# Three-block kernel on one core: the experts' weight chunks made whole and their ring one long strip, low parts of the dense weights written in place, the last dense loads on ScalarE's queue

## The reference, cut to what matters

```
hn = rmsnorm(h, ln_ffn[1])
logits = hn @ w_router;  top 2 of 8, softmax over the two -> combine[token, expert]
for e in range(8):
    g, u = split(hn @ w_gu[e])            # w_gu[e]: 1024 x 7168
    out += combine[:, e] * ((silu(g) * u) @ w_down[e])   # w_down[e]: 3584 x 1024
return rmsnorm(h + out, ln_final)
```

## Time and profile before

| | |
|---|---|
| median of 3 runs | 1381.46 us (1381.21 to 1382.87) |
| profiled execution, device time | 1384.53 us |
| its span, first to last instruction | 1382.8 us |
| TensorE / VectorE / ScalarE busy | 95% / 34% / 26% |
| DMA | 445.41 MB, mean 322 GB/s |
| mean granted TensorE clock | 0.990 |

### The profile page before, as it was taken

One profiled execution on the slowest core, in us unless ns is written; L12 is line 12 of the kernel. 1 busy time (PEld: TensorE's weight loads), 2 busy tenths in 40 slices (PEclk: granted clock), 3 DMA queues, 4 the chain that ended last, 5 costly groups with the idle time before them and its releaser, 6 DMA issues.

```text
span 1382.8 us, 29468 instructions
## 1 busy us (share of the span) xinstructions
PE 1320.2 (95%) x12866; PEld 804.5 (58%) x12866; DVE 471.6 (34%) x756; ACT 361.1 (26%) x524; POOL 37.7 (3%) x62
## 2 busy tenths in 40 slices
PE   9999999999999999999999998999988999988885
PEld 8678888887899987454345353345343345343242
DVE  7775555446689983320200200200200200200102
ACT  6754444335578853200000000000000000000001
POOL 1000000000002221000000000000000000000000
PEclk9999999999999999999999999999999999999997
DMA  9446555564644449899999999999999999999992
GB/s 351 135 153 213 183 184 182 184 203 130 201 134 126 150 183 369 350 424 425 425 425 424 424 424 425 424 425 425 423 426 425 423 425 424 425 425 426 421 424 116
DMA packets 112593, 445.41 MB, mean 322 GB/s; under 512 B 10400, under 2 KB 36272, under 8 KB 81744
## 3 DMA queue, kind: packets, MB, share of 16 engines
q1 hardware_dynamic: 109216, 440.44, 80.3%
q10 hardware_dynamic: 2912, 2.36, 0.5%
q0 software_dynamic: 336, 0.71, 0.2%
HBM read 442.43 MB, written 1.05 MB: 321 GB/s over the span
## 4 chain that ended last, share of the span: by engine, by line
PE 67%; SPq 14%; DMA 10%; DVE 4%; issue 2%; ACT 2%; DVEq 1%; ACTq 0%
PE bank L1302 22%; SPq L381 14%; PE bank L797 10%; PE bank L799 10%; PE bank L798 10%; PE bank L1318 9%; DMA e_ring<-moe_w_down_in 4%; DMA e_late<-moe_w_down_in 2%; DMA e_top<-moe_w_down_in 2%; DMA e_ring<-moe_w_gu_in 2%; PE bank L1292 1%; DVE w_lo L1441 1%; PE bank L1273 1%; ACT w_hi L504 1%; DVE acc L1777 1%
## 5 line engine op out<-in xcount | busy, mean ns | idle before, releaser
L1302 PE MATMUL bank<-e_ring,xgT 128*32 128x512 f32 (+1 forms) x3840 | 375.6, 540 | 8.8 <-DMA e_ring<-moe_w_gu_in 8.8
L1302 PEld LDWEIGHTS bank<-e_ring,xgT 128*32 128x32 f32 x3840 | 122.3, 110 | 251.8 <-issue 221.8
L1441 DVE TENSOR_TENSOR w_lo<-ring,w_hi 128x2048 fp32r<-128x2048 f32 (+1 forms) x84 | 191.8, 2288 | 108.3 <-ACT w_hi L504 108.0
L1318 PE MATMUL bank<-e_ring,m_hT 128*32 128x256 f32 x3344 | 194.6, 388 | 23.8 <-DMA e_ring<-moe_w_down_in 17.9
L504 ACT ACTIVATE w_hi<-ring 128x2048 fp32r<-128x2048 f32 (+1 forms) x84 | 158.9, 1894 | 127.5 <-PE bank L799 119.6
L1318 PEld LDWEIGHTS bank<-e_ring,m_hT 128*32 128x32 f32 x3344 | 111.8, 112 | 101.0 <-issue 28.9
L797 PE MATMUL bank<-w_hi,hT_hi 128*128 128x512 f32 (+1 forms) x336 | 130.7, 389 | 1.9 <-DVE w_lo L1441 1.9
L1998 DVE TENSOR_TENSOR m_sg<-m_sg,bank 128x512 f32<-128x512 f32 (+1 forms) x38 | 21.6, 617 | 321.8 <-PE bank L1302 321.8
L799 PE MATMUL bank<-w_hi,hT_lo 128*128 128x512 f32 (+1 forms) x336 | 129.2, 385 | 0.0
L798 PE MATMUL bank<-w_lo,hT_hi 128*128 128x512 f32 (+1 forms) x336 | 129.1, 384 | 0.0
L757 ACT ACTIVATE m_sg<-bank 128x512 f32<-128x512 f32 (+1 forms) x38 | 18.3, 543 | 374.1 <-PE bank L1302 374.1
(11 more groups left out here) (358 smaller groups left out, 1427.2 us busy)
## 6 DMA issues: line engine op xcount, KB each, us to landing
e_ring<-moe_w_gu_in SPq DMA_DIRECT2D x100, 1024.0 KB, 26.4
e_ring<-moe_w_down_in SPq DMA_DIRECT2D x88, 1024.0 KB, 24.5
e_ring<-moe_w_gu_in SPq DMA_DIRECT2D x101, 768.0 KB, 22.2
ring<-ffn_w_gu_in SPq DMA_DIRECT2D x28, 1024.0 KB, 5.1
ring<-ffn_w_down_in SPq DMA_DIRECT2D x14, 1024.0 KB, 4.9
e_top<-moe_w_gu_in SPq DMA_DIRECT2D x14, 1024.0 KB, 27.2
e_late<-moe_w_gu_in SPq DMA_DIRECT2D x14, 1024.0 KB, 26.9
e_top<-moe_w_down_in SPq DMA_DIRECT2D x12, 1024.0 KB, 24.4
```

Of the source, the lines that this page charges most:

```text
L1302: ins = pe.matmul(bank[banks[b]][quad_of(q), 0:w].rearrange("p (m v) -> p m v", v=P // 2), xgT[:, k, quad_of(b)], columns_of(e_slot(p * LA ...
L1318: ins = pe.matmul(bank[DOWN[b]][quad_of(q), 0:256], m_hT[:, 2 * c + k, rows], wv[:, columns], start=(c == 0 and k == 0), stop=(c == KT // ...
L1441: dve.tensor_tensor(w_lo[:, m % SPLIT, 0:w], ring[:, m % RING, 0:w], w_hi[:, m % SPLIT, 0:w].bitcast(F32), ALU.subtract).then_inc(lo_ready, 1)
```

## The change

Seven things change.

1. **Chunks of the experts.** A gate or up chunk is one whole row block, 128 x 3584 floats (14 KiB for each partition, 1.835 MB); a down chunk has four rows of 1024 for each partition (16 KiB, 2.097 MB). A pass has 23 chunks in place of 46: 8 gate, 8 up, 7 down.
2. **The ring.** One strip of 12 x 14 KiB = 168 KiB per partition in place of 19 x 8 KiB = 152 KiB. `expert_ring` lays the chunks end to end and notes for each the last chunk that it overwrites (`E_FREES`); 13 semaphores (`e_loaded`) follow the loads.
3. **The first lap.** Twelve chunks (22.0 MB) in place of 19 (19.1 MB). Their waits are others: three go after SyncE's last dense load, one at SO0, then at MOE0 - 5, MOE0 - 4 and MOE0 - 2, one once the norm is done, and the last four at MOE0, when TensorE has used the last dense chunk.
4. **The dense stage.** `w_lo` lies over `ring`, so that VectorE writes it in place, and a slot is reloaded after TensorE's use (`chunk_used`) and not after `w_lo`. The eight loads SO0 to MOE0 - 1 are issued by ScalarE in `ahead`, ahead of the rounding three chunks back.
5. **The order in a pass.** Each gate chunk goes through all banks of both sets, then each up chunk. Up goes over the gate banks, each once its silu is read (`m_silu`). `rows_next` stands ahead of `down`. `down` has banks of 512 columns.
6. **The start and the end.** The first expert matmul waits for all eight pieces of `xgT` (before: for the first four), and the last pass fills one bank of 512 columns per tile, copied in pieces of 32x512 (before: two banks, 32x256).
7. **Gains.** `ln_ffn` is loaded after MOE0 (before: before it), `ln_final` in the last pass (before: at 565 us).

```diff
+STRIP = 128
 SETS = ((0, 512), (4 * 512, 384))
-CONTIGUOUS = 15
-SLOT_OF = (17, 18, 13, 14, 15, 0, 1, 2, 3, 4, 5, 16, 6, 7, 8, 9, 10, 11, 12)
-ERING = len(SLOT_OF)
...
 KT = FF // P
-LAYER_CHUNKS = 32 + KT // 2
+GU_CHUNKS = 2 * KD
+DOWN_ROWS = 4
+LAYER_CHUNKS = GU_CHUNKS + KT // DOWN_ROWS
+FIRST_LAP = (2, 3, 4, 5, 6, 7, 8, 1, 9, 10, 11, 0)
+LANES = len(FIRST_LAP) + 1
+E_AT = 25600
+HT_AT = E_AT + len(FIRST_LAP) * 4 * FF - 96 * 1024
+
+
+def chunk_size(i):
+    return FF if i % LAYER_CHUNKS < GU_CHUNKS else DOWN_ROWS * D
+
+
+def expert_ring():
+    places, at, size = [], FIRST_LAP[0] * FF, len(FIRST_LAP) * FF
+    for i in range(ROUND_CHUNKS):
+        if i < len(FIRST_LAP):
+            places.append(FIRST_LAP[i] * FF)
+            continue
+        at = at if at + chunk_size(i) <= size else 0
+        places.append(at)
+        at += chunk_size(i)
+    frees = [max([i - LANES] + [j for j in range(i) if places[j] < places[i] + chunk_size(i)
+                                and places[i] < places[j] + chunk_size(j)]) for i in range(ROUND_CHUNKS)]
+    return places, frees
+
+
+E_PLACE, E_FREES = expert_ring()
...
+        def dense_load(queue, n):
+
+            width = sum(p[3] for p in stream[n])
+            for src, k, a, w in stream[n]:
+                dst = ring[:, n % RING, 0:k * width].rearrange("p (k n) -> p k n", n=width)
+                queue.dma_start(dst[:, :, a:a + w], src).then_inc(slot_loaded[n % RING], 16)
...
+        e_ring, = phase(E_AT, e_ring=((len(FIRST_LAP) * FF,), F32))
+        hT_hi, hT_lo, hT, ring, w_hi = phase(
+            HT_AT, hT_hi=((KD, T), F32R), hT_lo=((KD, T), F32R), hT=((KD, T), F32), ring=((RING, SLOT), F32),
+            w_hi=((SPLIT, SLOT), F32R))
+        _, _, decay_mov, decay_stat, after, ident_r, w_lo = phase(
+            HT_AT, under_hT_hi=((KD, T), F32), under_hT_lo=((KD, T), F32), decay_mov=((TT, REP, P), F32R),
+            decay_stat=((2, 3, P), F32R), after=((P,), F32R), ident_r=((P,), F32R), w_lo=((RING, SLOT), F32R))
...
-        GATE, UP, DOWN = (0, 1, 2), (3, 4, 5), (6, 7, 5)
-        FIRST_AT = [(6, 0), (5, 0), (5, 1), (4, 0), (4, 1), (4, 2), (3, 0), (3, 1)]
-        FIRST_DONE = (1, 2, 2, 3, 3, 3, 4, 4)
+        ROWS, DOWN = (0, 1), (6, 7)
+        FIRST_AT = [(6, 0), (5, 0), (5, 1), (5, 2), (2, 0), (2, 1), (2, 2), (2, 3)]
+        FIRST_DONE = (1, 2, 2, 2, 3, 3, 3, 3)
...
-            for n, pieces in enumerate(stream):
+            for n in range(SO0):
...
                 if n >= RING:
-                    sp.wait_ge(lo_ready, n - RING + 1)
-                for src, k, a, w in pieces:
-                    width = sum(p[3] for p in pieces)
-                    dst = ring[:, n % RING, 0:k * width].rearrange("p (k n) -> p k n", n=width)
-                    sp.dma_start(dst[:, :, a:a + w], src).then_inc(slot_loaded[n % RING], 16)
+                    sp.wait_ge(chunk_used, n - RING + 1)
+                dense_load(sp, n)
 
             def expert_load(e, i):
 
                 c = i % LAYER_CHUNKS
-                if c < 32:
-                    first, w = SETS[c // 16]
-                    a = c // 8 % 2 * FF + first
-                    src, n = block_of(moe_w_gu[0, e], c % 8, 1, a, BLOCKS * w), BLOCKS * w
+                if c < GU_CHUNKS:
+                    src = moe_w_gu[0, e][P * (c % KD):P * (c % KD + 1), c // KD * FF:(c // KD + 1) * FF]
                 else:
-                    rows = slice(2 * P * (c - 32), 2 * P * (c - 31))
-                    src, n = moe_w_down[0, e][rows].rearrange("(p k) n -> p k n", k=2), 2 * D
-                dst = e_slot(i)[:, 0:n].rearrange("p (k n) -> p k n", k=src.shape[1])
-                sp.dma_start(dst, src).then_inc(e_loaded[i % ERING][0], 16)
+                    rows = slice(DOWN_ROWS * P * (c - GU_CHUNKS), DOWN_ROWS * P * (c - GU_CHUNKS + 1))
+                    src = moe_w_down[0, e][rows].rearrange("(p r) n -> p (r n)", r=DOWN_ROWS)
+                sp.dma_start(e_slot(i), src).then_inc(e_loaded[i % LANES], 16)
 
...
                 sp.wait_ge(c_dt_parts, 4)
-                for i in range(2):
+                for i in range(3):
                     expert_load(0, i)
                 sp.wait_ge(chunk_used, SO0)
-                for i in range(2, 4):
-                    expert_load(0, i)
+                expert_load(0, 3)
+                sp.wait_ge(c_abx, G)
+                sp.wait_ge(chunk_used, MOE0 - 5)
+                expert_load(0, 4)
+                sp.wait_ge(chunk_used, MOE0 - 4)
+                expert_load(0, 5)
+                sp.wait_ge(chunk_used, MOE0 - 2)
+                expert_load(0, 6)
                 sp.wait_ge(c_y, G)
-                expert_load(0, 4)
-                for r in range(RING):
-                    sp.wait_ge(lo_ready, MOE0 + r - RING + 1)
-                    expert_load(0, 5 + r)
                 sp.wait_ge(c_yThi, KI)
                 sp.wait_ge(c_yTsb, KI)
                 sp.wait_ge(c_norm, 1)
-                expert_load(0, 5 + RING)
-                for r in range(2 * SPLIT):
-                    sp.wait_ge(chunk_used, MOE0 + r % SPLIT - SPLIT + 1)
-                    expert_load(0, 6 + RING + r)
-                sp.wait_ge(r_mm, 4)
-                expert_load(0, ERING - 1)
+                expert_load(0, 7)
+                sp.wait_ge(chunk_used, MOE0)
+                for i in range(8, len(FIRST_LAP)):
+                    expert_load(0, i)
...
-                    for i in range(max(p * LAYER_CHUNKS, ERING), (p + 1) * LAYER_CHUNKS):
-                        sp.wait_ge(chunk_used, it * ROUND_CHUNKS + (MOE0 + i - ERING + 1))
+                    for i in range(max(p * LAYER_CHUNKS, len(FIRST_LAP)), (p + 1) * LAYER_CHUNKS):
+                        sp.wait_ge(chunk_used, it * ROUND_CHUNKS + (MOE0 + E_FREES[i] + 1))
...
+                    if SO0 <= m + RING - SPLIT < MOE0:
+                        dense_load(act, m + RING - SPLIT)
...
+            act.wait_ge(chunk_used, MOE0)
+            act.dma_start(ffn_gain, ln_ffn[1].partition_broadcast(P)).then_inc(ffn_gain_loaded, 16)
...
-                def up_or_gate(c, s, banks):
-                    w, k = SETS[s][1], c % 8
+                def up_or_gate(c, passed, free=None):
+
+                    k, at = c % KD, hidden_banks(p)
                     have_e(c)
-                    for b in range(groups):
+                    for i, (s, b) in enumerate(at):
+                        if free and k == 0:
+                            pe.wait_ge(free, it * banks_before(E) + (banks_before(p) + i + 1))
                         for q in range(BLOCKS):
...
+                            ins = pe.matmul(hidden_bank(s, b)[quad_of(q)].rearrange("p (m v) -> p m v", v=STRIP),
+                                            xgT[:, k, quad_of(b)], columns_of(e_slot(p * LAYER_CHUNKS + c), s, q),
                                             start=(k == 0), stop=(k == KD - 1), tile_position=(0, q * QUAD))
+                        if k == KD - 1 and i < len(at) - 1:
+                            ins.then_inc(passed, 1)
                     ins.then_inc(chunk_used, 1)
 
...
+                def down(c):
+
+                    have_e(GU_CHUNKS + c)
+                    last = c == KT // DOWN_ROWS - 1
+                    for b in range(groups - 1):
+                        for r in range(DOWN_ROWS):
+                            wv = e_slot(p * LAYER_CHUNKS + GU_CHUNKS + c)[:, r * D:(r + 1) * D]
+                            for q in range(4):
+                                rows, columns = down_at(b, q)
+                                ins = pe.matmul(bank[DOWN[b]][quad_of(q), 0:columns.stop - columns.start],
+                                                m_hT[:, DOWN_ROWS * c + r, rows], wv[:, columns],
+                                                start=(c == 0 and r == 0), stop=(last and r == DOWN_ROWS - 1),
+                                                tile_position=(0, q * QUAD))
+                        if last and b < groups - 2:
                             ins.then_inc(m_y, 1)
-
+                    ins.then_inc(chunk_used, 1)
+
+                pe.wait_ge(xg_sb, it * (2 * E) + (2 * p + 2))
...
+                    up_or_gate(KD + k, m_up, m_silu)
                 if p == 0:
                     pe.wait_ge(rows_ready, TT)
                 pe.wait_ge(pass_sel, it * E + (p + 1))
-                pe.wait_ge(m_h, it * (2 * E) + (2 * p + 2))
+                pe.wait_ge(m_h, it * (2 * E) + (2 * p + 1))
                 rows_next()
-                for c in range(4, 8):
-                    down((c,))
+                if p == 0:
+                    pe.wait_ge(rows_held, it + 1)
+                else:
+                    pe.wait_ge(h_added, it * (2 * TT * E) + (2 * TT * p + 2 * TT))
+                pe.wait_ge(m_T, it * (2 * E) + (2 * p + 1))
+                for c in range(4):
+                    down(c)
                 pe.wait_ge(m_T, it * (2 * E) + (2 * p + 2))
-                for c in range(8, 12):
```

(37 more changed lines are left out.)

268 lines of the change are left out of this document (127 added, 141 removed).

## The result

The changed kernel takes 1374.96 us (median of 5 runs, 1374.0 to 1375.08); the kernel before, on the same chip, 1382.28 (5 runs, 1381.21 to 1383.2). The ratio is 0.9946, with a 95% interval of 0.9931 to 0.9960: 7.3 us faster, where 18.1 were forecast, and outside the range. The profiled execution had a span of 1373.3 us and took 1375.08 in all.

The account below looks back on a forecast made before the run. The prediction took the expert stage to be one long DMA transfer at 420 to 426 GB/s, with TensorE not its bound. Terms 7.8 + 8.6 + 2.5 - 0.8 = 18.1 us turned 1381.46 into 1363.4 us, range 1353 to 1374.

Parts of the forecast that it names:

- B: Expert stage's transfer rate: 1432 fewer packets per DMA engine at 6 ns each, 8.6 us gained, bounds 5.6 and 15.0.
- A: Start of the expert stage: more bytes moved before the DMA engines are full, 7.8 us gained.
- D: Tail after the last down matmul: the final matmul waits for one 32x512 copy, 0.8 us lost.
- So 1.05 MB more is there, 2.5 us: Before 549 us: eight loads, 14.7 MB, issued early against thirteen, 13.6 MB; 2.5 us gained at 425 GB/s.
- What does a packet cost beside its bytes?: Expert loads: packet times of 8 and 6 KiB gave 3.9 to 10.5 ns fixed cost; 6 was taken.
- the page's 5.0 us: Expert-stage rate: alternative estimate from the Trainium skill's page, 3 cycles or 3.5 ns per packet, 5.0 us gained.
- C: Last expert chunk: waited for alone, TensorE's clock holds and its work takes about 3.5 us; 2.5 us gained.
- Costs put at nothing: Dense and expert stages: ScalarE's DMA issues (2.8 us if uncovered), later slot reloads, `ln_ffn`, reordered passes; all hidden.
- packets were not cut: Rival, expert loads: 14 and 16 KiB packets are cut at 8 KiB, no rate gain, 1372.0 us; chance 0.10.
- the dense stage ended: Rival: dense stage ends later or TensorE starts late, 2.8 uncovered and 3 more, 1369.2 us; chance 0.08.
- rows of 16 KiB: Rival, down loads: 16 KiB rows are slow, gain gone at 399 GB/s, bound near 1510 us; chance 0.04.
- the clock held: Rival: TensorE's clock falls in lock-step at idle times of 1.5 us, about 1371 us; chance 0.04.

Follow-up runs that it names:

- x7: The changed kernel with expert loads 8 to 11 also waiting until TensorE has counted the chosen tokens: 1380.74 us, ratio 0.9989 to the kernel before.
- x1: The changed kernel with every expert load issued as two loads of half its width (packets of 7 and 8 KiB): 1387.39 us, ratio 1.0033.
- y2: The kernel before with its buffers moved in SBUF, the expert ring starting 448 bytes past a multiple of 512: 1395.39 us, ratio 1.0093.
- x3: The kernel before, with TensorE waiting for the last two down chunks of an expert separately instead of together: 1379.97 us, ratio 0.9979.
- x8: The changed kernel with the last down chunk loaded as four one-row loads, each used when it has landed: 1372.34 us, ratio 0.9922.
- y5: y1 with the last down chunk also loaded and used row by row: 1366.60 us, ratio 0.9883 to the kernel before.
- w_two_rows: y1 with the last down chunk in four rows and the one before it in two halves: 1366.98 us, ratio 0.9889.
- y3: y1 with every expert load issued as two halves (packets of 7 and 8 KiB): 1375.14 us, ratio 0.9947 to the kernel before.
- y1: The aligned run: the changed kernel with the expert ring starting at a multiple of 512 bytes instead of 448 past one: 1367.47 us, ratio 0.9896.
- z2: y1 with 4,004 more GpSimd instructions that nothing waits for, spread over the expert stage: 1374.22 us, ratio 0.9937.

## Why the prediction was wrong

The forecast was 18.1 us and 7.3 came. The step that failed is in B, the rate: it took the price of a packet from rows of a ring that starts on a multiple of 256 bytes, and the new ring's start, which no term names, cost 7.5 us. Beside that A was 3.6 us too large, B's size 0.9, and D 1.3 too small; 2 to 3 us came that no term had.

**What bounds the kernel** was read rightly: moving bytes later (x7), a slower rate (x1, y2) and a shorter tail (x3, x8) each showed in the time. Gains of about 1 us at the tail (y5, w_two_rows) were too small to tell.

**A, 7.8 us, was mis-sized.** What it said of 549 to 573 us was nearly right: 405 GB/s for 310 are 2.28 MB, 5.4 us of the 6.5 forecast. The step "So 1.05 MB more is there, 2.5 us" failed. It counted loads issued, thirteen against eight. But a load issued at 543.82 had also mostly moved by 549: in the trace both kernels have moved the same expert bytes by then, 14.80 and 14.79 MB. With the gain's 1.2 us off, A is 4.2 us.

**B, 8.6 us, is 7.7 on an aligned ring (y3 against y1), but in the changed kernel most of it was eaten.** The failed step is the silent one behind "What does a packet cost beside its bytes?": that a packet costs in the new ring what the rows of the old ring show. The ring's start moved off a multiple of 256 bytes, and that took 7.5 us back (y1 against the changed kernel). Nothing in the profile of before could price it, but the allocation could be read off the two kernels, and was an edit like any other; it wasn't in my list, not even at nothing. (A slip in the text of B: with the page's 5.0 us the total would be 14.5, not 14.3, in place of 18.1, not 17.9.)

**C, 2.5 us, was right:** 2.4 by the rows (3.64 us of work on the last chunk for 6.01), and the granted clock stayed at 1.00 in lock-step with waits of 1.2 to 1.7 us. x3 shows the mechanism by itself.

**D, 0.8 us, was too small:** from the last down matmul's end to the span's end were 12.7 us (1382.8 - 1370.1) and are 14.8 (1373.3 - 1358.5), 2.1 more. 0.9 is the wait for the copy, as worked out, 0.8 the fall of the clock within the last eight matmuls (4.51 in place of 3.67 us), the rest are small pieces. The prediction had the clock hold, but hadn't asked until when. That fall doesn't come every time: x1 and x7, with the same tail, had 3.67.

**Costs put at nothing** stayed so. The router's matmuls come 0.5 us later (547.82 against 547.33), which is no more than two profiles of one code differ by.

**What wasn't seen:** that a load lands with its slowest engine, and that engines drift apart. The last engine's lag behind the mean of 8.3 us (7.6 in x3's profile) became 6.0, and 5.5 on the aligned ring: some 2 us gained by no term. It isn't the size of packets, since with halves on the aligned ring the lag is 5.4. There are fewer instructions to fetch (87 packets in queue 8, before 102); that the fetches make this part of the drift wasn't tested, and z2 shows only that more of them add to it.

The sum again, on the aligned ring: 4.2 + 7.7 + 2.4 - 1.2 (D with the clock up, 13.9 - 12.7) + 2 to 3 (lag 7.6 to 8.3, now 5.5) = 15 to 16 us; measured 1382.84 - 1367.47 = 15.4, by the ratio 14.4. Less the 7.5 between the aligned and the changed kernel it is about 8, and the changed kernel gained 7.3.

**The rivals.** None happened: packets were not cut, the dense stage ended at most 0.5 us later and not 5.8, rows of 16 KiB ran at full rate, and the clock held. The sign was right; the case that came wasn't among them.

## What to carry to other kernels

When a kernel is bound by DMA, put the start of every large buffer that it fills on a multiple of 256 bytes and look at it again after each change of layout: here 32 bytes and the order of two tables were worth 7.5 us, as much as the whole change. A packet's duration that scatters where it used to be one value is the sign. Count a load as landed when its slowest engine is done, and keep code that nothing needs off the engines in a long transfer, GpSimd's above all.

## What the runs showed of the hardware

- A packet of 8192 B takes 309 ns and one of 16384 B 611 when its place in SBUF starts on a multiple of 256 bytes; off it 3 to 6 ns more on average. In the changed kernel, 192 bytes past a multiple, half of the packets pay 2 or 3 ns and a fifth 9 or 10.
- Halving packets of 14 and 16 KiB costs 5.2 ns for each one more, by the kernel's time.
- One core alone read 428 GB/s from DRAM for 767 us (the aligned run, 573 to 1340 us).
- The 16 DMA engines of a core drift apart in a long transfer, to 12 to 16 us between first and last over 800 us here, and extra GpSimd code (29 packets of 8 KiB) put one engine 6 us behind all others.
